# The last layer norm of a two-block transformer kernel: its eight tiles divided among three engines

## The reference, cut to what matters

```python
DEEPNORM_ALPHA = (2 * DEPTH_2) ** 0.25
LN_EPS = 1e-5

def layer_norm(x, g, b):
    xf = x.astype(jnp.float32)
    mu = xf.mean(-1, keepdims=True)
    var = jnp.square(xf - mu).mean(-1, keepdims=True)
    return ((xf - mu) * lax.rsqrt(var + LN_EPS) * g + b).astype(x.dtype)

def second_block(...):
    ...
        ff = grouped_moe(x, router_w, router_bias, w_gate[l], w_up[l], w_down[l])
        x = layer_norm(DEEPNORM_ALPHA * x + ff, ln_moe_g[l], ln_moe_b[l])
    return x
```

## Time and profile before

| | |
|---|---|
| time, median of 3 runs | 2457.43 us (2453.64 to 2457.77) |
| the profiled execution: its time, its span | 2458.28 us, 2456.9 us |
| busy over the span: PE, DVE, ACT, POOL | 95%, 51%, 24%, 26% |
| last landing of the experts' sums, first load issued | 2427.30 us |
| the first tile of the last stage starts, the last VectorE instruction starts | 2430.61 us, 2452.94 us |

### The profile page before, as it was taken

One profiled execution on the slowest core, in us unless ns is written; L12 is line 12 of the kernel. 1 busy time (PEld: TensorE's weight loads), 2 busy tenths in 40 slices (PEclk: granted clock), 3 DMA queues, 4 the chain that ended last, 5 costly groups with the idle time before them and its releaser, 6 DMA issues.

```text
span 2456.9 us, 25964 instructions
## 1 busy us (share of the span) xinstructions
PE 2346.2 (95%) x9779; PEld 1370.9 (56%) x9779; DVE 1249.6 (51%) x2584; ACT 582.8 (24%) x1345; POOL 636.3 (26%) x528
## 2 busy tenths in 40 slices
PE   8999999999999999999999999999999999699993
PEld 5676657764444444444444677744464644488772
DVE  5444425444567777877753466665501336511124
ACT  3344423321122221222211111111100221011113
POOL 1000000044543454453272000007341045112213
PEclk9999999999999999999999999999999999799997
DMA  5000210122110110110235201003250213658987
GB/s 171 1 1 1 86 35 1 47 68 86 35 35 18 35 35 18 35 35 20 93 87 157 70 13 44 34 1 139 101 199 7 69 46 141 211 148 263 274 248 215
DMA packets 145211, 203.88 MB, mean 83 GB/s; under 512 B 16820, under 2 KB 101684, under 8 KB 145080
## 3 DMA queue, kind: packets, MB, share of 16 engines
q1 hardware_dynamic: 138168, 176.99, 21.9%
q0 software_dynamic: 6912, 25.17, 4.3%
HBM read 164.37 MB, written 37.77 MB: 82 GB/s over the span
## 4 chain that ended last, share of the span: by engine, by line
PE 85%; POOL 3%; DVE 3%; DMA 2%; issue 2%; ACT 1%; POOLq 0%; DVEq 0%; ACTq 0%
PE banks L171 79%; PE banks L174 6%; DMA arena<-x_scratch,slots 1%; POOL arena L1430 1%; POOL arena L1448 1%; DVE arena L3806 0%; DVE arena L3813 0%; DVE arena L896 0%; POOL arena L1425 0%; POOL arena L1431 0%; DMA x_scratch<-arena,places 0%; POOL arena L1433 0%; POOL x_scratch L3519 0%; POOL arena L1459 0%; ACT arena L3138 0%
## 5 line engine op out<-in xcount | busy, mean ns | idle before, releaser
L171 PE MATMUL banks<-arena 128*128 128x512 f32 (+16 forms) x8131 | 2183.9, 456 | 30.2 <-DVE arena L3374 5.7
L171 PEld LDWEIGHTS banks<-arena 128*128 128x128 f32 (+6 forms) x8131 | 1197.3, 183 | 920.6 <-issue 831.3
L174 PE MATMUL banks<-arena 128*128 128x128 f32 (+2 forms) x1552 | 222.2, 280 | 41.5 <-DVE arena L448 10.4
L174 PEld LDWEIGHTS banks<-arena 128*128 128x128 f32 (+2 forms) x1552 | 178.6, 142 | 113.8 <-issue 66.1
L2161 POOL TENSOR_TENSOR arena<-arena 128x512 f32<-128x512 f32 (+3 forms) x160 | 154.5, 967 | 166.4 <-ACT arena L1972 146.7
L259 POOL TENSOR_TENSOR arena<-arena 128x1 f32<-128x1 f32 (+1 forms) x88 | 65.0, 741 | 486.0 <-DVE arena L2697 312.0
L1425 POOL TENSOR_TENSOR arena<-arena 128x512 f32<-128x512 f32 x4 | 9.3, 2321 | 572.7 <-PE banks L174 453.2
L1972 ACT ACTIVATE arena<-arena 128x512 f32<-128x512 f32 (+4 forms) x160 | 81.6, 576 | 315.7 <-DVE arena L2063 314.5
L2031 DVE TENSOR_TENSOR arena<-arena 128x512 f32<-128x512 f32 (+3 forms) x160 | 106.4, 723 | 28.3 <-ACT arena L1964 28.3
L3519 POOL DMA_INDIRECT x_scratch<-arena,places x24 | 37.8, 1577 | 204.4 <-DVE arena L3672 204.4
L2063 DVE TENSOR_TENSOR arena<-arena,banks 128x512 f32<-128x512 f32 (+4 forms) x160 | 89.5, 624 | 1.1 <-PE banks L174 1.1
(11 more groups left out here) (346 smaller groups left out, 1735.0 us busy)
## 6 DMA issues: line engine op xcount, KB each, us to landing
x_scratch<-arena SPq DMA_DIRECT2D x40, 512.0 KB, 2.9
arena<-in_o_w_in_dram SPq DMA_DIRECT2D x32, 512.0 KB, 5.4
arena<-x_scratch SPq DMA_DIRECT2D x32, 512.0 KB, 5.4
arena<-in_w_gate_dram SPq DMA_DIRECT2D x16, 1024.0 KB, 14.8
arena<-in_w_up_dram SPq DMA_DIRECT2D x16, 1024.0 KB, 17.3
arena<-in_w_down_dram SPq DMA_DIRECT2D x16, 1024.0 KB, 19.8
arena<-in_x_dram SPq DMA_DIRECT2D x16, 512.0 KB, 5.0
arena<-in_w_in_dram SPq DMA_DIRECT2D x16, 512.0 KB, 7.0
```

What stands on the lines that cost most here:

```text
L171: return pe.matmul(o, a, b, start=start, stop=stop)
L174: return pe.transpose(o, a, ident)
```

## The change

Both halves of the norm's algebra stay; who does what changes.

- Tiles 0, 2 and 4 ("by GpSimd"): VectorE takes mean and variance by `bn_stats`/`bn_aggr` and negates the mean; GpSimd adds epsilon, raises to minus one half, and makes minus mean times root; ScalarE makes tile times root plus that (`Identity` with scale and bias); GpSimd multiplies by the gain row and adds the bias row, both over 128x1024.
- Tiles 1, 3, 5, 6, 7 ("by VectorE"): as before, but ScalarE's copy carries the scale -1/D, so the one-element instruction goes, and GpSimd also adds the epsilon before each root.
- ScalarE copies the two rows into PSUM banks 0 to 3 (`GAIN`, `BIAS`), in four pieces, before it waits for the last sums; VectorE reads them there.
- The order of roots is 0, 2, 1, 3, 4, 5, 6, 7, that of stores 1, 0, 3, 2, 5, 6, 4, 7. The small columns of each tile get their own 32 words (`LS`). The first four load events are old semaphores used again.

```diff
+        LS = [scr(40, 256)[:, 32 * t:32 * t + 32] for t in range(NT)]
+        GAIN, BIAS = bank(0, 2), bank(2, 2)
+        BY_POOL, BY_DVE, ROOTS = (0, 2, 4), (1, 3, 5, 6, 7), (0, 2, 1, 3, 4, 5, 6, 7)
+        pool_th, dve_th, root_th = BY_POOL.index, BY_DVE.index, ROOTS.index
...
-            for t in range(NT):
-                Y.wait_ge(xn_done, fin.xn + t + 1)
+            for t in (1, 0, 3, 2, 5, 6, 4, 7):
+                if t in BY_POOL:
+                    Y.wait_ge(pool_out, pool_th(t) + 1)
+                else:
+                    Y.wait_ge(xn_done, fin.xn + dve_th(t) + 1)
                 sync.dma_start(out[0][128 * t:128 * t + 128, :], LAST[t]).then_inc(d_out.sem, 16)
...
+        def pool_last_root(t):
+            s, i = LS[t], fin.eps + root_th(t) + 1
+            if t in BY_POOL:
+                G.wait_ge(last_bn, pool_th(t) + 1)
+                pool.tensor_scalar(s[:, 3:4], s[:, 21:22], 1.0, LN_EPS / ALPHA ** 2, MUL, ADD).then_inc(eps_done.sem, 1)
+                G.wait_ge(eps_done, i)
+                gl(root(s[:, 4:5], s[:, 3:4]))
+                gl.done()
+                pool.tensor_tensor(s[:, 5:6], s[:, 22:23], s[:, 4:5], MUL).then_inc(pow_done.sem, 1)
+            else:
+                G.wait_ge(last_sq, dve_th(t) + 1)
+                pool.tensor_scalar(s[:, 3:4], s[:, 2:3], 1.0 / D, LN_EPS / ALPHA ** 2, MUL, ADD).then_inc(eps_done.sem, 1)
+                G.wait_ge(eps_done, i)
+                root(s[:, 4:5], s[:, 3:4]).then_inc(pow_done.sem, 1)
+        def pool_last_gain(t):
+            G.wait_ge(last_normed, pool_th(t) + 1)
+            gl(pool.tensor_tensor(LAST[t], LAST[t], XB[0], MUL))
+        def pool_last_bias(t):
+            gl.done()
+            pool.tensor_tensor(LAST[t], LAST[t], XB[1], ADD).then_inc(pool_out.sem, 1)
...
+        def act_last_stats(t):
+            s, i = LS[t], dve_th(t)
+            C.wait_ge(d_fin[t], 16)
+            C.wait_ge(last_sq, i - 1)
+            act.activation(YS[2 * i % 3], OTf[t], ACT.Copy, scale=-1.0 / D, accum_out=s[:, 1:2]).then_inc(mean_known.sem, 1)
+            C.wait_ge(mean_known, i + 1)
+            act.activation(YS[(2 * i + 1) % 3], OTf[t], ACT.Square, bias=s[:, 1:2], accum_out=s[:, 2:3]).then_inc(last_sq.sem, 1)
+        def act_last_norm(t):
+            C.wait_ge(d_fin[t], 16)
+            C.wait_ge(pow_done, fin.pow + root_th(t) + 1)
+            act.activation(LAST[t], OTf[t], ACT.Identity, bias=LS[t][:, 5:6], scale=LS[t][:, 4:5]).then_inc(last_normed.sem, 1)
...
+            for dst, src in ((GAIN, XB[0]), (BIAS, XB[1])):
+                for h in range(2):
+                    act.activation(dst[:, 512 * h:512 * h + 512], src[:, 512 * h:512 * h + 512], ACT.Copy)
+            C.wait_ge(d_put, 384)
...
+        def dve_last_moments(t):
+            s = LS[t]
+            V.wait_ge(d_fin[t], 16)
+            for h in range(2):
+                vs(vec.bn_stats(s[:, 8 + 6 * h:14 + 6 * h], OTf[t][:, 512 * h:512 * h + 512]))
+            vs.done()
+            vs(vec.bn_aggr(s[:, 20:22], s[:, 8:20]))
+            vs.done()
+            vec.tensor_scalar(s[:, 22:23], s[:, 20:21], -1.0, None, MUL).then_inc(last_bn.sem, 1)
+        def dve_last_gain(t):
+            V.wait_ge(mean_known, dve_th(t) + 1)
+            vec.scalar_tensor_tensor(LAST[t], OTf[t], LS[t][:, 1:2], GAIN, ADD, MUL).then_inc(last_gain.sem, 1)
         def dve_last_out(t):
...
+            vec.scalar_tensor_tensor(LAST[t], LAST[t], LS[t][:, 4:5], BIAS, MUL, ADD).then_inc(xn_done.sem, 1)
         def dve_last():
...
+            dve_last_moments(0)
+            dve_last_gain(1)
+            dve_last_moments(2)
+            dve_last_out(1)
+            dve_last_gain(3)
+            dve_last_moments(4)
+            dve_last_out(3)
+            dve_last_gain(5)
+            dve_last_out(5)
+            dve_last_gain(6)
+            dve_last_gain(7)
+            dve_last_out(6)
+            dve_last_out(7)
```

More of the change, by code:

```diff
@@ L3767, in program @@
         mean_known, last_sq, last_gain = event("mean_known"), event("last_squares"), event("last_gained")
+        last_bn, last_normed = event("last_moments"), event("last_normed")
+        pool_scaled, pool_out = event("last_scaled_by_pool"), event("last_out_by_pool")
+        gl = Chain(pool, pool_scaled.sem)
         fin = Step(False)
-        d_fin = [event(f"sum_landed_{t}") for t in range(NT)]
+        d_fin = [d.again() for d in (*d_x, d_sn[0])] + [event(f"sum_landed_{t}") for t in range(4, NT)]
         d_out = event("output_stored")
         LAST = [HT[:, t, :] for t in range(NT)]
+        LS = [scr(40, 256)[:, 32 * t:32 * t + 32] for t in range(NT)]
+        GAIN, BIAS = bank(0, 2), bank(2, 2)
+        BY_POOL, BY_DVE, ROOTS = (0, 2, 4), (1, 3, 5, 6, 7), (0, 2, 1, 3, 4, 5, 6, 7)
+        pool_th, dve_th, root_th = BY_POOL.index, BY_DVE.index, ROOTS.index
         def sp_last():
@@ L3778, in sp_last @@
                 load(OTf[t], x5[128 * t:128 * t + 128, :], d_fin[t])
-            for t in range(NT):
-                Y.wait_ge(xn_done, fin.xn + t + 1)
+            for t in (1, 0, 3, 2, 5, 6, 4, 7):
[3 more added lines that the diff above has]
+                    Y.wait_ge(xn_done, fin.xn + dve_th(t) + 1)
                 sync.dma_start(out[0][128 * t:128 * t + 128, :], LAST[t]).then_inc(d_out.sem, 16)
             Y.wait_ge(d_out, 16 * NT)
-        def pool_last():
[L3785 to L3788, removed]
@@ L3790, in act_last @@
-        def act_last():
[L3791 to L3800, removed]
+        def pool_last_root(t):
[12 more added lines that the diff above has]
+                root(s[:, 4:5], s[:, 3:4]).then_inc(pow_done.sem, 1)
@@ new lines, in pool_last_gain @@
+        def pool_last_gain(t):
[4 more added lines that the diff above has]
+            pool.tensor_tensor(LAST[t], LAST[t], XB[1], ADD).then_inc(pool_out.sem, 1)
+        def pool_last():
+            G.wait_ge(d_g, g_moe + 32)
+            for t in (0, 2, 1):
+                pool_last_root(t)
+            pool_last_gain(0)
+            pool_last_bias(0)
+            pool_last_root(3)
+            pool_last_gain(2)
+            pool_last_bias(2)
+            pool_last_root(4)
+            pool_last_root(5)
+            pool_last_gain(4)
+            pool_last_root(6)
+            pool_last_bias(4)
+            pool_last_root(7)
@@ new lines, in act_last @@
+        def act_last():
+            C.wait_ge(d_g, g_moe + 32)
+            C.wait_ge(ht_done, 16)
+            C.wait_ge(ys_a, 24)
+            C.wait_ge(ys_v, 24)
+            for dst, src in ((GAIN, XB[0]), (BIAS, XB[1])):
+                for h in range(2):
+                    act.activation(dst[:, 512 * h:512 * h + 512], src[:, 512 * h:512 * h + 512], ACT.Copy)
+            C.wait_ge(d_put, 384)
+            act_last_stats(1)
+            act_last_norm(0)
+            act_last_stats(3)
+            act_last_norm(2)
+            act_last_stats(5)
+            act_last_norm(4)
+            act_last_stats(6)
+            act_last_stats(7)
@@ L3802, in dve_last_out @@
         def dve_last_out(t):
[L3803 to L3806, removed]
+            V.wait_ge(pow_done, fin.pow + root_th(t) + 1)
+            V.wait_ge(last_gain, dve_th(t) + 1)
+            vec.scalar_tensor_tensor(LAST[t], LAST[t], LS[t][:, 4:5], BIAS, MUL, ADD).then_inc(xn_done.sem, 1)
         def dve_last():
-            V.wait_ge(d_g, g_moe + 32)
```

## The result

The changed kernel takes 2462.59 us (median of 20 runs, 2458.09 to 2465.24); the kernel before, run on the same chips, 2457.3 us (20 runs, 2452.84 to 2459.2). The ratio is 1.0023, 95% interval 1.0016 to 1.003: slower by 5.3 us between the medians, about 5.7 by the ratio. The forecast was 2461.6 us in 2458.0 to 2465.5. The profiled execution's span is 2462.6 us long, 5.7 more than that of the kernel before (2456.9 us).

The account below looks back on a forecast made before the run. The prediction took GpSimd's queue as the new bound: the stage ends at 27.4 us instead of 23.6, 3.8 later, plus 0.4 for the stores, 4.2 on the median 2457.43, giving 2461.6 us, range 2458.0 to 2465.5.

Parts of the forecast that it names:

- The mechanism: In the last norm stage the bound moves from VectorE to GpSimd, PSUM rows end their contention, end 3.8 us later.
- The costs of GpSimd: GpSimd per instruction: 2.35 us full width, 0.18 us one column, 0.55 us a root; its whole work 21.4 us.
- Rival 1: GpSimd's one-column instructions cost as much as a root, 0.55 us: +7.1 us in all, 2464.5 us; chance 0.14.
- rival 3: GpSimd's two-input instructions run at its copy's pace, 1.2 us a tile: 2455.8 us; chance 0.10.
- the queue: GpSimd's instructions followed in time order with waits, to VectorE's last bias ending at 27.4 us, against 23.6 before.
- The moments of tile 2: VectorE's mean and variance of tile 2, behind the gain of tile 1: ending at 5.4 us, GpSimd waiting for them.
- A root between full-width instructions: GpSimd's epsilon, wait and root for a VectorE tile: 0.18 + 0.08 + 0.55 = 0.81 us.
- ScalarE's scaling: ScalarE's scaling of a full GpSimd tile: 1.05 us each, taken from the 1.04 us of the copy.
- The tail: Stores after the last computing instruction: tiles 6 and 4 finish close before tile 7, adding 0.4 us, out of 0 to 1.
- The library reload: Reload at the head of GpSimd's block: any load hidden by ten microseconds of GpSimd idling before its first epsilon.
- Rival 2: GpSimd's library is loaded at first use, not at the reload, a stall of up to 5 us: 2464.0 us; chance 0.06.
- the waits in the order: GpSimd idle from 2.9 to 5.5 us, and ScalarE's sums of tiles 6 and 7 behind its scaling of tile 4.

Follow-up runs that it names:

- e1: The kernel before, all eight tiles on VectorE, with only the gain and bias rows copied to PSUM and read there: stage 23.1 us against 23.6.
- e2: The changed kernel with VectorE reading gain and bias rows from SBUF again, the PSUM copies staying unread: stage 35.2 us against 28.6.
- e4: The changed kernel with GpSimd's three bias additions (tiles 0, 2, 4) left out: stage 22.7 us against 28.6, tail 4.1 us.
- e3: The changed kernel's same work with roots, GpSimd's queue, ScalarE's last sums and stores reordered: stage 25.0 us against 28.6, ratio to the kernel before 1.0004.

## Why the prediction came out as it did

**The mechanism was right.** The bound moved to GpSimd, PSUM rows keep the engines apart (e1, e2), and the stage ended later. That the kernel is slower is clear of the noise. On which side of 0.2% it lies is not: the ratio is 0.23% above 1, its interval 0.16 to 0.30%, and the prediction had put 0.54 on "within 0.2%" and 0.40 on slower. The forecast was +4.2 us; the stage and tail give +5.0 and +0.6, 5.6 in sum, and the ratio says the same.

**The costs of GpSimd held.** Full width 2.35 predicted, 2.36 and 2.35 measured; one column 0.18 against 0.19; a root 0.55 against 0.55. The straight line through additions of 128 and 2048 columns gave the price of a multiplication of 1024, which no row had. Rival 1 (small ones as dear as a root) and rival 3 (the pace of a copy) fall with these rows.

**The term that was mis-sized is the queue, 27.4 us predicted and 28.6 measured.** Following it instruction by instruction:

- The moments of tile 2 ended at 5.7 in place of 5.4. About half of this is its late landing, at 3.95 (2434.67 us) and not 2.7: VectorE was free at 3.8 and began at 4.0. The rest is the gain ahead of it, 0.06 us late and 0.07 us longer than predicted. The prediction spread the loads evenly over 9.3 us; in this execution the longest took 10.2 us from issue to landing. In the others it was 9.1 to 11.0 us, with 10.6 in e1, where the loads are those of before, which speaks for scatter and not for the change.
- A root between full-width instructions of GpSimd took 0.91 us (2443.27 to 2444.18 us), not 0.81: the first of its two waits was not counted. Roots 2, 1, 3, 4, 6 and 7 on the chain made some 0.6 us of this.
- ScalarE's scaling with scale and bias took 1.23 us, not the 1.05 of the plain copy; with its waits the link from root 4 to gain 4 is 0.25 us longer.
- VectorE's last instruction took 1.28 us and not 1.21. The row was a tensor_tensor with one input in banks; the scalar_tensor_tensor of full width has not become shorter by PSUM.

These give 0.3 + 0.6 + 0.25 + 0.07, the missing 1.2.

**The tail** was 0.6 longer, 0.4 being predicted, and the reason given fits: tiles 6 and 4 go out just ahead of tile 7 (finished at 2457.29, 2457.11 and 2459.34 us). In e4, where three stores go out within 1.6 us (tile 4 was done at 2446.87 us but stood behind tile 6 in the order of stores), it is 4.1 us; in single file (e3) it is 2.6.

**The library reload** took 476 ns at 2422.1 us, ten microseconds ahead of the first epsilon, and this took 0.19 us like all others. Rival 2 is out. The Trainium skill ("GPSIMD Engine Reference", section "2.1 Instruction dispatch") has the first call to a freshly loaded kernel pay a load of 5.95 us; no such pause shows here, either because nothing new had to be loaded or because it ended within GpSimd's 10.04 us of waiting. These runs don't tell which.

**What the waits in the order cost.** The prediction named them (GpSimd idle from 2.9 to 5.5, ScalarE's last sums behind the scaling of tile 4) but counted them into the forecast without asking what an order without them would give; e3, which takes both away and spreads the roots, puts 3.6 us on the order as a whole.

## What to carry to other kernels

Add up the new owner's whole queue before giving it work, small instructions and waits included: here GpSimd's 21 us against VectorE's former 20 said before the first run that three tiles were too many. In a queue of instructions that wait for other engines, one that waits for late work (ScalarE's scaling of tile 4) should stand behind those that don't. When a division gains, undo it and keep its side parts: here moving a 0.15 us instruction to an idle engine, sparing ScalarE another and taking an operand from PSUM gave 2.2 us of the 2.8 us that the best division found. And look at every engine that is full, not only at the one that the chain names: before, ScalarE ran at the same 2.55 us a tile as VectorE.

## What the runs showed of the hardware that was not expected

- GpSimd at 128x1024 float32 multiplies and adds at the same pace, 2.36 and 2.35 us, next to 4.51 us for an addition of 128x2048 and 453 ns for one of 128x128: linear in the columns within 1%.
- The exclusion reaches the one-column instructions too. In e2 the five `L3805` took 705 ns on the mean, against 192 in the changed kernel, and VectorE's full-width ones 2.36 and 2.48 us on the mean against 1.28.
- Behind the branch ScalarE began its copies to PSUM only at 2425.89 us, 5.7 us after its last evacuation had ended at 2420.2 us. The copies ended at 2428.04 us, 0.5 us behind the last landing of the sums, so the wait that the prediction named as their cover did not quite hide them; the loads did, since ScalarE's first sum came 4.0 us later still. In the other runs with these copies the pause ahead of them was 4.0 to 5.3 us:

```profile
2419.53 0.69 ACT L3645 ACTIVATE arena<-banks,arena 128x512 f32<-128x512 f32 x1 [2.91 <-PE banks L171]
2425.89 2.15 ACT L3853 ACTIVATE banks<-arena 128x512 f32<-128x512 f32 x4 [5.68 <-issue]
```

What filled the 5.7 us, the branch or the fetch of what stands behind it, was not tried.
